# The first expert's rows: picked with the matrix of ones as weights, then transposed

## The reference, cut to what matters

```
h2 = rmsnorm(x, norm2_g) * (1 + scale2) + shift2
combine = ...    # [512, 16], two nonzero weights a token
for e in range(16):
    act = silu(h2 @ w_gate[e]) * (h2 @ w_up[e])
    out = out + combine[:, e:e+1] * (act @ w_down[e])
```

## Time and profile before

| | us |
|---|---|
| median of 3 runs | 1576.24 |
| lowest and highest | 1574.02, 1576.59 |
| the profiled execution | 1571.04 |
| its span | 1569.2 |
| TensorE busy | 1523.2 (97%) |
| VectorE busy | 895.3 (57%) |
| ScalarE busy | 744.9 (47%) |
| GpSimd busy | 736.9 (47%) |

### The profile page before, as it was taken

The page is one execution under the profiler, slowest core; times in us unless marked ns, Lnnn a source line. Parts: engine busy times, 40 slices in busy tenths (PEclk is TensorE's granted clock), DMA queues, the critical chain, the costliest instruction groups (busy, mean ns, idle before and its releaser), DMA issues.

```text
span 1569.2 us, 19745 instructions
## 1 busy us (share of the span) xinstructions
PE 1523.2 (97%) x7391; PEld 1202.1 (77%) x7391; DVE 895.3 (57%) x1458; ACT 744.9 (47%) x1183; POOL 736.9 (47%) x463
## 2 busy tenths in 40 slices
PE   8998999999999999999998999999999899999997
PEld 6675656787888888888887777777888688888885
DVE  5358987134133694756635323432002599999998
ACT  5226877223243323232243563532224378888885
POOL 4256666443575655555455573653546255111100
PEclk9999999999999999999999999999999999999999
DMA  7420000422323555554332331221236299999974
GB/s 254 130 99 28 1 1 14 142 94 85 103 82 134 214 188 190 191 196 181 117 98 67 109 121 55 68 81 55 94 97 230 106 365 390 397 383 384 380 306 176
DMA packets 75085, 251.31 MB, mean 160 GB/s; under 512 B 11747, under 2 KB 13091, under 8 KB 74984
## 3 DMA queue, kind: packets, MB, share of 16 engines
q1 hardware_dynamic: 67408, 234.93, 41.2%
q0 software_dynamic: 4752, 8.11, 1.4%
q10 hardware_dynamic: 2824, 6.94, 1.2%
HBM read 245.47 MB, written 12.66 MB: 164 GB/s over the span
## 4 chain that ended last, share of the span: by engine, by line
PE 85%; DVE 6%; POOL 3%; issue 2%; ACT 2%; DMA 2%; SPq 1%; DVEq 0%; POOLq 0%; ACTq 0%
PE ps L428 17%; PE ps L432 16%; PE ps L429 16%; PE ps L966 3%; PE ps L962 3%; PE ps L963 3%; PE ps L450 2%; PE ps L454 2%; PE ps L451 2%; PE ps L995 2%; PE ps L991 2%; PE ps L992 2%; PE ps L645 1%; PE ps L774 1%; PE ps L611 1%
## 5 line engine op out<-in xcount | busy, mean ns | idle before, releaser
L302 POOL TENSOR_TENSOR RS<-RAW,RS 128x1024 fp32r<-128x1024 f32 x174 | 433.8, 2496 | 434.4 <-ACT RS L297 419.8
L297 ACT ACTIVATE RS<-RAW 128x1024 fp32r<-128x1024 f32 x306 | 321.3, 1056 | 238.2 <-PE ps L432 147.1
L428 PE MATMUL ps<-RH,RS 128*128 128x512 f32 x816 | 323.1, 396 | 9.9 <-ACT RS L297 7.2
L432 PE MATMUL ps<-RH,RS 128*128 128x512 f32 x816 | 319.0, 391 | 0.4 <-POOL RS L302 0.4
L429 PE MATMUL ps<-RH,RS 128*128 128x512 f32 x816 | 318.6, 390 | 0.0
L428 PEld LDWEIGHTS ps<-RH,RS 128*128 128x128 f32 x816 | 153.9, 189 | 44.6 <-ACT RS L297 9.0
L432 PEld LDWEIGHTS ps<-RH,RS 128*128 128x128 f32 x816 | 153.7, 188 | 33.8 <-POOL RS L302 0.8
L429 PEld LDWEIGHTS ps<-RH,RS 128*128 128x128 f32 x816 | 153.9, 189 | 32.3 <-issue 1.2
L302 DVE TENSOR_TENSOR RS<-RAW,RS 128x1024 fp32r<-128x1024 f32 x132 | 154.4, 1220 | 9.6 <-ACT RS L297 9.4
L428 PE MATMUL ps<-RA,RS 128*128 128x512 f32 x400 | 156.3, 391 | 0.0
L429 PE MATMUL ps<-RA,RS 128*128 128x512 f32 x400 | 155.7, 389 | 0.0
(11 more groups left out here) (378 smaller groups left out, 2668.0 us busy)
## 6 DMA issues: line engine op xcount, KB each, us to landing
RAW<-in_w_ff SPq DMA_DIRECT2D x64, 512.0 KB, 4.5
RAW<-in_w_gate SPq DMA_DIRECT2D x46, 512.0 KB, 8.6
RAW<-in_w_up SPq DMA_DIRECT2D x43, 512.0 KB, 8.5
RAW<-in_w_down SPq DMA_DIRECT2D x41, 512.0 KB, 8.3
PB<-in_ada SPq DMA_DIRECT2D x24, 512.0 KB, 3.7
TB<-in_ada SPq DMA_DIRECT2D x24, 512.0 KB, 3.7
RAW<-in_w_gb SPq DMA_DIRECT2D x16, 512.0 KB, 3.3
RAW<-in_w_ga SPq DMA_DIRECT2D x16, 512.0 KB, 3.3
```

Source lines behind the costliest of these rows:

```text
L297: act.activation(RS[:, spl[n], 0, :], raws[slot[n]], ACT.Copy).then_inc(*HI.up(n))
L302: eng.tensor_tensor(RS[:, s, 1, :], raws[slot[n]], hif(RS[:, s, 0, :]), ALU.subtract).then_inc(*mark.up(n))
L428: pe.matmul(b[:, :], wh, xh, start=(k == 0), stop=False)
L432: last = pe.matmul(b[:, :], wl, xh, start=False, stop=(k == K - 1))
```

## The change

TensorE no longer picks and transposes in one step. `PICK[0]` is now the weights and 512 columns of `HROWS` move: `first_rows` makes two halves of the picked rows, four matmuls each, in banks 2 and 3. ScalarE copies each half to `PC` (`evict`), and TensorE transposes the rows from there as it does for the other units. The second expert's list is made in the middle of the second half. On VectorE the copy of the list stands right behind the copy of `rank`; `rows_lo(0, 0)` stands behind `base` and `rows_lo(0, 1)` behind `mm`, where `rows_lo(0, 0)` was; the call of `prep(0)` before `weights()` is gone.

```diff
--- before.py
+++ after.py
@@ -913,10 +913,6 @@
         last.then_inc(*P.up("rank"))
 
 
-        def second_list():
-
-            slot_list("list", 1)
-
         def slot_list(key, u):
             b = take(key, (7,))
             pe.wait_ge(*V(("pick", u)))
@@ -924,27 +920,31 @@
                 last = pe.matmul(b[:, 0:1], PICK[1][i], RG["tk"][:, i:i + 1], start=(i == 0), stop=(i == 3))
             last.then_inc(*P.up(key))
 
+        def first_rows():
+
+            for hf in range(2):
+                b = take(("pk", hf), (2 + hf,))
+                if hf == 0:
+                    pe.wait_ge(*V(("pick", 0)))
+                pe.wait_ge(*V(("row", 3, hf)))
+                for i in range(4):
+                    if hf == 1 and i == 2:
+                        slot_list("list", 1)
+                    last = pe.matmul(b[:, :], PICK[0][i], HROWS[i][:, 512 * hf:512 * hf + 512], start=(i == 0), stop=(i == 3))
+                last.then_inc(*P.up(("pk", hf)))
+
         def prep(u):
+            if u == 0:
+                first_rows()
+            rows_ = flat(PC[:, 0:2, :]) if u == 0 else XIN1 if u == 1 else XIN[u % 2]
             for hf in range(2):
                 b = take(("xt", u, hf), (hf,))
-                if u == 0 and hf == 0:
-                    pe.wait_ge(*V(("pick", u)))
                 if u == 0:
-                    pe.wait_ge(*V(("row", 3, hf)))
+                    pe.wait_ge(*A(("ev", ("pk", hf))))
                 elif hf == 0:
                     pe.wait_ge(*(XS if u < 16 else XE)[u % 2](u))
-                for k in range(4):
-                    c = (4 * hf + k) * 128
-                    if u:
-                        rows_ = XIN1 if u == 1 else XIN[u % 2]
-                        last = pe.transpose(b[:, 128 * k:128 * k + 128], rows_[:, c:c + 128], identf[:, :])
-                        continue
-                    if hf == 0 and k == 3:
-                        second_list()
-                    for i in range(4):
-                        last = pe.matmul(b[:, 128 * k:128 * k + 128], HROWS[i][:, c:c + 128], PICK[0][i],
-                                         start=(i == 0), stop=(i == 3))
-                last.then_inc(*P.up(("xt", u, hf)))
+                transposes(b, [(b[:, 128 * k:128 * k + 128], rows_[:, 512 * hf + 128 * k:512 * hf + 128 * k + 128])
+                               for k in range(4)], ("xt", u, hf))
 
         def up(u, name, bi):
             d = XH[u % 2]
@@ -1459,10 +1459,12 @@
         for i in range(4):
             act.wait_ge(*V(("row", i, 1)))
             act.dma_start(t["hs"][128 * i:128 * i + 128, :], HROWS[i]).then_inc(*HST.up("all"))
+        evict(("pk", 0), PC[:, 0, :])
         act.wait_ge(*V("gx"))
         act.activation(RG["gx"], RG["gx"], ACT.Exp).then_inc(*A.up("gx"))
         act.wait_ge(*V("ex"))
         act.activation(RG["ex"], RG["ex"], ACT.Exp).then_inc(*A.up("ex"))
+        evict(("pk", 1), PC[:, 1, :])
 
 
         def prep(u):
@@ -2271,6 +2273,8 @@
         rtt(RG["gx"], G3, b3(RG["gm"], 4), ALU.subtract, "gx")
         rtt(RG["ex"], RG["es"], b3(RG["m1"], 4), ALU.subtract, "ex")
         rcopy(rank, ps["rank"][:, 0:80], ("ev", "rank"))
+        dve.wait_ge(*P("list"))
+        rcopy(SLOT1[:, :], ps["list"][:, 0:1], "list", ("ev", "list"))
         rts(xe, rank[:, 64:80], 128.5, None, ALU.is_gt)
         for lim in (256.5, 384.5):
             rstt(xe, rank[:, 64:80], lim, xe, ALU.is_gt, ALU.add)
@@ -2281,14 +2285,13 @@
         base, mm = RG["base"], RG["mm"]
         rstt(base, xi, 15.0, xe, ALU.add, ALU.subtract)
         rtt(base, base, EXP, ALU.subtract)
-        dve.wait_ge(*P("list"))
-        rcopy(SLOT1[:, :], ps["list"][:, 0:1], "list", ("ev", "list"))
+        rows_lo(0, 0)
         R3, V3, M3 = (a.rearrange("p (i e) -> p i e", i=4) for a in (rank[:, 0:64], RG["vl"], mm))
         rts(mm, rank[:, 0:64], 127.5, None, ALU.is_gt)
         rtt(V3, M3, base.unsqueeze(1).broadcast_to([128, 4, 16]), ALU.mult)
         for lim in (255.5, 383.5):
             rstt(mm, rank[:, 0:64], lim, mm, ALU.is_gt, ALU.add)
-        rows_lo(0, 0)
+        rows_lo(0, 1)
         rstt(V3, M3, 1.0 - 128.0 * NUNIT, V3, ALU.mult, ALU.add)
         rstt(V3, R3, float(NUNIT), V3, ALU.mult, ALU.add)
         rtt(V3, V3, EXP.unsqueeze(1).broadcast_to([128, 4, 16]), ALU.add)
@@ -2336,8 +2339,7 @@
 
         def prep(u):
             for hf in range(2):
-                if u or hf:
-                    rows_lo(u, hf)
+                rows_lo(u, hf)
 
         def tiles(name, u, between=None):
             for c in range(4):
@@ -2361,9 +2363,10 @@
             tt(AH[u % 2][:, 1, :], ps["at", u], hif(AH[u % 2][:, 0, :]), ALU.subtract, ("ev", ("at", u)), ("ah", u))
 
         def experts(u0, u1):
-            prep(u0)
             if u0 == 0:
                 weights()
+            else:
+                prep(u0)
             for u in range(u0, u1):
                 last = u == u1 - 1
                 if last:
```

## The result

The changed kernel takes 1579.0 us in the median of 20 runs (1576.91 to 1581.99), the kernel before, timed beside it, 1574.47 us (20 runs, 1570.59 to 1578.1). The ratio is 1.0029 with a 95% interval of 1.0021 to 1.0036, which is +4.6 us (+3.3 to +5.7). It is slower, by more than the 0.2% that can be told from no change. The forecast was +5.8 us (1582.0 us, range 1578.6 to 1585.8).

What follows compares the result with a forecast made beforehand. The prediction took VectorE's chain of small dependent routing instructions, not TensorE, as the bound. It summed 4.8 (chain) + 1.7 (clock) - 0.7 (old gather wait) = +5.8 us on 1576.24 us: 1582.0 us, range 1578.6 to 1585.8.

Steps and rivals of the forecast that it cites:

- The pick: TensorE's eight 512-column pick matmuls: 0.427 us a record at full clock, the second list finished 2.5 us later.
- The rule of the Trainium skill: Rival at the picks: a 512-column record advances in half of 0.427 us, giving +1.9 us, 1578.1 us; chance 0.05.
- The copies and transposes: ScalarE's two added copies and TensorE's eight transposes after the picks: first w_gate matmul starts 1.93 us later.
- VectorE's chain: Routing chain waits for list and ScalarE's hi half; tile (0,3)'s lo half comes late, TensorE resumes 4.8 us later.
- The clock: TensorE's clock falls after the 4.4 us wait at tile (0,3), 3.4 us at half speed: 1.7 us lost.
- GpSimd's queue: Scatters and the gather of unit 2's rows, behind `pos`, come 5.4 us later; the gather is just covered.
- The old wait of 0.7 us: TensorE's wait for gathered rows at unit 2's transposes goes away: -0.7 us.
- The sum: Whole kernel: 4.8 (VectorE's chain) + 1.7 (clock) - 0.7 (old gather wait) = +5.8 us.

Runs made afterwards that it cites:

- e5: Changed kernel with the second list made ahead of the picks' second half, its copy behind mm, both rows_lo(0, .) behind the third pick; 1.0000 against the kernel before.
- e1: Changed kernel with the second list made ahead of the second half of the picks, not in its middle; 1.0027 against the kernel before.
- e6: Changed kernel with only the two rows_lo(0, .) moved behind the third pick on VectorE; 1.0037 against the kernel before.
- e3: Changed kernel with 17 needless 512-column matmuls just ahead of TensorE's wait for the lo half of tile (0,3); 1.0026 against the kernel before.
- e2: Changed kernel with VectorE's copy of the list behind the cast of POS and both rows_lo(0, .) behind the third pick; 1.0014 against the kernel before.
- e7: Kernel before with both rows_lo(0, .) moved behind the third pick and weights() behind the copy of list2; 1.0013 against the kernel before.
- e4: Kernel before with the second list moved from behind the twelfth of 32 pick matmuls to behind the 24th; 1.0014 against the kernel before.
- e8: e3 with VectorE copies of 256 PSUM columns behind each split of unit 0's w_up and unit 1's first three of w_gate; 1.0061 against the kernel before.

## Why the prediction was right

**The pick.** Forecast: 0.427 us a record, the list finished 8.08 us behind the first pick. Measured: 0.427 us and 8.15 us. The price per column read from two other shapes carried over. It is the difference of the two durations, 0.85 ns a column; the prediction's words that 273 and 599 ns a record are as much a column for both forms are wrong as they stand (2.13 and 1.17 ns), and what is equal is the distance from start to start, 0.88 and 0.83 ns a column. The rule of the Trainium skill that would have made wide matmuls twice as cheap a column (TensorE: Matmul & The Clock Gate, "Back-to-back issue gap") does not hold for these float32 products: 0.112 us a record for 128 columns, 0.427 us for 512.

**The copies and transposes.** w_gate 1.93 us later by forecast, 2.1 us measured. In the changed kernel the longer wait at tile (0,3) hides it, and e5 shows that it costs nothing even without that wait.

**VectorE's chain.** rows_lo(0, 0) forecast 11.19 us behind the first pick, measured 11.27; `pos` 15.83 and 15.76; L302 19.88 and 20.03; TensorE's wait 4.4 and 4.42 us. What the prediction told too simply is which wait counts: it said that everything is queued behind the list, but e1 shows that the list alone is worth nothing here, and e6 that the hi half alone is worth 1.4 us of L302's delay (1.8 us with the clock's earlier rise). The sum was right, since it followed the chain through both.

**The clock.** Forecast 3.4 us at half, loss 1.7 us; measured 3.4 us and 1.6 us in the first profile, and a fall in all three. What one would get back by keeping it up is less, 0.3 to 0.6 us by e3's profile, because there the gather ends a wait.

**GpSimd's queue.** This step came out right by luck. The gather was to be issued 5.4 us later and be just covered. It started only 1.5 us later, because the eighth scatter took 1.66 us instead of 5.06 us, which the prediction did not expect. The result would have been the same without that: in e3, where the scatter and the gather took 5 us each, the rows were there 44.49 us behind the first pick, and the changed kernel's TensorE came for them at 45.25. The old wait of 0.7 us went as forecast.

**The sum.** +5.8 us forecast; +5.6 us behind the first pick in the first profile, +5.5 us over the mean of three and two profiles, +4.6 us (3.3 to 5.7) in the medians. Term by term the first profile has +5.0 (the end of the wait at tile (0,3)), +1.6 (clock), -0.7 (the old wait for the gather) and -0.2 that no term of the forecast stands for. The profiles agree with the sum, and the interval of the medians takes them in; the medians lie a little under it. Single executions of one kernel reach the first pick at very different times (1251.3 and 1253.2 us before, 1253.9, 1255.8 and 1257.4 us after), which is as large as the effect; whether the missing 1 us is anything but this spread is open. The forecast of 1582.0 us is 3 us over the measured 1579.0 us, and 1.8 us of that is the base: I had put the difference on a median of three runs, 1576.24 us, and 20 runs gave 1574.47 us.

## What to carry to other kernels

When a copy is moved up in a chain where every instruction waits for the last, follow the chain through all its gates before pricing one: two waits in a row hide each other, and opening either gate alone gained nothing in the times here (1.0027 and 1.0037 against 1.0029). Taking both out of the chain gave half of it back (e2, 1.0014), and all of it (e5, 1.0000) once the list was early enough for the gather that hangs on it. A change on the busiest engine can be free where it fills a wait that was there (the wide picks, two copies, eight transposes and a start 2 us later cost nothing in e5) and expensive on the engine that runs beside it. A repair has to be checked for what it makes late: e2 cured the chain and starved a gather, e7 emptied one gap and filled another.

## What the runs showed of the hardware that was not expected

Two of GpSimd's indirect transfers, the eighth scatter and the gather of unit 2, took three to four times as long where they lay beside a burst of VectorE's splits without a gap. The bursts, in the kernel before and in e3:

```profile
1273.21 4.61 DVE L302 TENSOR_TENSOR RS<-RAW,RS 128x1024 fp32r<-128x1024 f32 x4
```

```profile
1281.49 4.61 DVE L302 TENSOR_TENSOR RS<-RAW,RS 128x1024 fp32r<-128x1024 f32 x4
```

In the kernel before the eighth scatter started at 1273.61 and ended at 1278.67; the four splits ran from 1273.21 to 1277.82. In e3 the splits ran from 1281.49 to 1286.10 and the scatter ended at 1286.94. Each time the transfer's issue ended 0.85 us behind the burst, and so it did in e4 (scatter 5.06 us) and e5 (gather 5.08 us). With a gap after the first split (0.38 us in the changed kernel, 0.19 us in e1) or copies on PSUM of 0.41 us between them (e8), the same scatter took 1.66 us. In the second profile of the kernel before, the fourth split started 0.1 us late, and the scatter (3.94 us) ended 0.86 us behind the third. The fourth and fifth scatters also lie under such a burst, and took 1.70 and 1.97 us in the kernel before, so a burst alone is not the whole condition; what else it takes was not tried.

The clock's stretch at half after a wait was 3.4 us after a wait of 4.42 us (changed kernel), and 6.8 us, the first 1.3 us of it still in the wait, with one of 3.88 us (e6). It did not fall at all after two waits of 1.27 and 1.81 us with matmuls between them (e4), nor after 1.46 and 0.60 us (second profile of the kernel before), but it did in e2, where the waits were 0.59 and 1.33 us. The length of the last wait alone does not tell.
